# Attention with VectorE, ScalarE and TensorE shifted by one score map

## What is computed

```python
# hybrid mixer: 8 heads, query and key width 96, value width 64, causal
s = jnp.einsum('bqhd,bkhd->bhqk', qi, k[:, :kv_len]) * scale
p = jax.nn.softmax(jnp.where(mask, s, -jnp.inf), axis=-1)
outs.append(jnp.einsum('bhqk,bkhd->bqhd', p, v[:, :kv_len]))

# even layer, differential attention: 4 heads, each with two maps, value width 128
s = jnp.einsum('bqhmd,bkhmd->bhmqk', q_blk, k) + bias[None, :, None]
p = jax.nn.softmax(jnp.where(visible, s, NEG_INF), axis=-1)
w = p[:, :, 0] - lam * p[:, :, 1]
out = jnp.einsum('bhqk,bkhd->bqhd', w, v)
# even layer, band attention: 8 heads of width 64, one map each
p = jax.nn.softmax(s + bias + mask, axis=-1)
out = jnp.einsum('bhnqk,bnkhd->bnqhd', p, vb)
```

## Time and profile before

| | us |
|---|---|
| median of 3 runs | 3531.28 (3527.48 to 3535.3) |
| profiled execution, its own time | 3538.57 |
| its span | 3536.8 |
| TensorE busy | 3287.1 (93%) |
| VectorE busy | 1962.2 (55%) |
| ScalarE busy | 1193.7 (34%) |
| GpSimd busy | 1003.5 (28%) |
| mean granted clock of TensorE over the span | 0.96 |

### The profile page before, as it was taken

One profiled execution on the slowest core, in us unless ns is written; L12 is line 12 of the kernel. 1 busy time (PEld: TensorE's weight loads), 2 busy tenths in 40 slices (PEclk: granted clock), 3 DMA queues, 4 the chain that ended last, 5 costly groups with the idle time before them and its releaser, 6 DMA issues.

```text
span 3536.8 us, 40413 instructions
## 1 busy us (share of the span) xinstructions
PE 3287.1 (93%) x14349; PEld 2589.3 (73%) x14349; DVE 1962.2 (55%) x2865; ACT 1193.7 (34%) x1790; POOL 1003.5 (28%) x713
## 2 busy tenths in 40 slices
PE   6999999999999999998999989988999978599998
PEld 4887875678787888775788767756878857378887
DVE  5565465656545533555655443347676479764443
ACT  3222244432223222425422223354333243143332
POOL 2888000068803700000188400000884021000000
PEclk9999999999999999999999999989999999799999
DMA  6666352166534633330366433202664332023332
GB/s 208 198 195 180 91 133 56 38 178 200 177 96 137 191 95 92 88 85 24 108 199 197 131 89 107 72 1 77 202 194 145 94 103 77 13 82 93 98 95 83
DMA packets 577201, 417.68 MB, mean 118 GB/s; under 512 B 30123, under 2 KB 537370, under 8 KB 575942
## 3 DMA queue, kind: packets, MB, share of 16 engines
q1 hardware_dynamic: 532434, 283.99, 27.4%
q0 software_dynamic: 34304, 121.64, 11.5%
q10 hardware_dynamic: 10356, 10.69, 1.1%
HBM read 408.91 MB, written 6.06 MB: 117 GB/s over the span
## 4 chain that ended last, share of the span: by engine, by line
PE 59%; DVE 16%; POOL 15%; issue 4%; ACT 3%; DMA 2%; ACTq 0%; SPq 0%; DVEq 0%; POOLq 0%
PE bank L324 17%; PE bank L326 17%; PE bank L325 17%; POOL mod_acc L663 8%; POOL mod_w L660 4%; PE bank L1264 2%; PE bank L1295 2%; POOL mod_w L632 2%; DVE tmp L438 2%; DMA mod_w<-in_w_ada 2%; DVE w_lo L305 2%; DVE h_lo L448 1%; POOL mod_acc L666 1%; PE bank L1285 1%; DVE w_lo L296 1%
## 5 line engine op out<-in xcount | busy, mean ns | idle before, releaser
L324 PE MATMUL bank<-h_hi,w_hi 128*128 128x512 f32 x2656 | 1053.5, 397 | 70.3 <-DVE w_lo L305 23.5
L326 PE MATMUL bank<-h_hi,w_lo 128*128 128x512 f32 x2656 | 1043.5, 393 | 0.0
L325 PE MATMUL bank<-h_lo,w_hi 128*128 128x512 f32 x2656 | 1043.3, 393 | 0.0
L305 DVE TENSOR_TENSOR w_lo<-raw,w_hi 128x1024 fp32r<-128x1024 f32 x438 | 660.7, 1509 | 538.1 <-ACT w_hi L288 535.9
L288 ACT ACTIVATE w_hi<-raw 128x1024 fp32r<-128x1024 f32 x438 | 462.1, 1055 | 671.6 <-PE bank L326 668.2
L324 PEld LDWEIGHTS bank<-h_hi,w_hi 128*128 128x128 f32 x2656 | 503.0, 189 | 208.1 <-issue 49.0
L326 PEld LDWEIGHTS bank<-h_hi,w_lo 128*128 128x128 f32 x2656 | 502.8, 189 | 108.4
L325 PEld LDWEIGHTS bank<-h_lo,w_hi 128*128 128x128 f32 x2656 | 503.6, 190 | 103.0 <-issue 0.2
L663 POOL TENSOR_TENSOR mod_acc<-mod_acc,mod_w 128x1024 f32<-128x1024 f32 x168 | 455.7, 2712 | 14.0
L324 PE MATMUL bank<-hid_hi,w_hi 128*128 128x512 f32 x1056 | 416.3, 394 | 15.4 <-DVE w_lo L305 15.3
L326 PE MATMUL bank<-hid_hi,w_lo 128*128 128x512 f32 x1056 | 414.2, 392 | 0.0
(11 more groups left out here) (318 smaller groups left out, 3350.1 us busy)
## 6 DMA issues: line engine op xcount, KB each, us to landing
raw<-in_ffn_w_gu SPq DMA_DIRECT2D x176, 512.0 KB, 4.0
mod_w<-in_w_ada POOLq DMA_DIRECT2D x128, 512.0 KB, 4.0
mod_w<-in_mod_w POOLq DMA_DIRECT2D x96, 512.0 KB, 4.2
raw<-in_ffn_w_in SPq DMA_DIRECT2D x88, 512.0 KB, 3.7
raw<-in_ffn_w_down SPq DMA_DIRECT2D x64, 512.0 KB, 4.0
raw<-in_w_in SPq DMA_DIRECT2D x34, 512.0 KB, 3.7
raw<-in_ffn_w_out SPq DMA_DIRECT2D x32, 512.0 KB, 4.0
raw<-in_ffn_w_down SPq DMA_DIRECT2D x32, 384.0 KB, 3.4
```

The lines of the kernel that those rows point to most:

```text
L305: loop(nc.vector.tensor_tensor(w_lo[:, u % 2, :], raw[:, u % 2, :], w_hi[:, u % 2, :].bitcast(F32), ALU.subtract), "split_lo", times)
L324: nc.tensor.matmul(dst, a_hi, b_hi, start=start, stop=False)
L325: nc.tensor.matmul(dst, a_hi, b_lo, start=False, stop=False)
L326: return nc.tensor.matmul(dst, a_lo, b_hi, start=False, stop=stop)
```

## The change

It shifts VectorE and ScalarE by one map and TensorE's scores by another:

- TensorE issues the scores of maps 0 and 1 at the start. In the turn of map j it transposes map j, issues the scores of map j + 2 and then the outputs of map j. For a map without outputs it only issues the scores of map j + 2.
- VectorE takes map j + 1 and then divides map j.
- ScalarE does the exponentials of map j + 1 and the evacuation of map j - 1 before the copies of map j.
- The latent stages get a third map buffer, `m_probs2`, at `mod_at`, with its slot in `smx`; a buffer is reused after three maps instead of two.

```diff
@@ -1172,6 +1172,7 @@
         m_later = [g[0]]
         m_probs = [place(f"m_probs{i}", [P, 1280], F32, m_later) for i in range(2)]
         m_probs_end = m_later[0]
+        m_probs.append(place("m_probs2", [P, 1280], F32, [mod_at]))
         lat = place("lat", [P, 6, S], F32, g)
         pos = place("pos", [P, S], I32, [g[0]])
         conv_u = place("conv_u", [P, S], F32, g)
@@ -1267,11 +1268,11 @@
 
             outs = [j for j in range(len(jobs)) if "v" in jobs[j]]
             scores(0)
+            scores(1)
             for j in range(len(jobs)):
-                if j + 1 < len(jobs):
-                    scores(j + 1)
                 job = jobs[j]
                 if "v" not in job:
+                    scores(j + 2)
                     continue
                 pb = job["turn"]
                 former = outs.index(j) - 1
@@ -1286,6 +1287,8 @@
                                                   ident[:, :])
                     if kb != 2:
                         done(ins, "probs_turned", (key, j, sig))
+                if j + 2 < len(jobs):
+                    scores(j + 2)
                 if job.get("free") is not None:
                     wait(pe, *job["free"])
                 rows, bank = job["rows"], job["bank"]
@@ -1311,6 +1314,10 @@
             exps(0)
             for j in range(len(jobs)):
                 job = jobs[j]
+                if j + 1 < len(jobs):
+                    exps(j + 1)
+                if j >= 1 and "v" in jobs[j - 1]:
+                    after(act, j - 1)
                 if "v" in job:
                     for g in range(3):
                         wait(act, "probs_turned", (key, j, g))
@@ -1321,12 +1328,9 @@
                         bank, c, _ = TURN_AT[g]
                         done(nc.scalar.activation(pt[:, g, g * P:S], psum[bank][:, c:c + n], ACT.Copy), "turned_read",
                              (key, j, g))
-                if j + 1 < len(jobs):
-                    exps(j + 1)
-                if "v" in job:
-                    after(act, j)
                 if beside is not None:
                     beside(act, j)
+            after(act, len(jobs) - 1)
 
         def attend_dve(dve, key, jobs, minus_lam=None, beside=None):
 
@@ -1366,9 +1370,9 @@
                     dve.wait_ge(sg.sem("probs_ready"), sg.count["probs_ready"])
             scores(0)
             for j in range(len(jobs)):
-                divide(j)
                 if j + 1 < len(jobs):
                     scores(j + 1)
+                divide(j)
                 if beside is not None:
                     beside(dve, j)
 
@@ -1428,8 +1432,8 @@
             for h in range(HEADS):
                 jobs.append(dict(
                     q=lambda i, h=h: q_full[0:HD, h, i * P:(i + 1) * P], k=lambda n, h=h: k_full[0:HD, h, 0:n],
-                    bias=causal, scale=HD ** -0.5, buf=m_probs[h % 2], slot=h % 2, turn=m_probs[h % 2],
-                    after=h - 2 if h >= 2 else None,
+                    bias=causal, scale=HD ** -0.5, buf=m_probs[h % 3], slot=h % 3, turn=m_probs[h % 3],
+                    after=h - 3 if h >= 3 else None,
                     v=lambda kb, h=h: v_tok[:, kb, h * VD:(h + 1) * VD], pt=m_probs_t,
                     rows=slice(VD * (h % 2), VD * (h % 2 + 1)), bank=h // 2 % 2))
             return jobs
```

## The result

| | before | after |
|---|---|---|
| median, us (4 runs each) | 3533.24 | 3565.96 (3554.83 to 3567.55) |
| ratio, 95% interval | | 1.0089 (1.0064 to 1.0113) |
| profiled execution, us | 3538.57 | 3567.20 |
| TensorE busy, us | 3287.1 | 3294.5 |
| mean granted clock | 0.96 | 0.954 |

Slower by 32.7 us: 3566 where 3570 was forecast. The windows view gives the three stages and two periods of four maps in the even stage (start:end, length, busy us of TensorE, its weight loads, VectorE, ScalarE and GpSimd, then clock, DMA share, GB/s). It answers to the earlier trace rows.

What follows compares the result with a forecast made beforehand. TensorE alone was taken to bound the steady latent stage. Two latent stages at +8.6 (+17.2) and the even stage at +21.2 gave +38.4: profiled 3577, median 3570, range 3550 to 3590.

Steps and rivals of the forecast that it cites:

- The ring: Latent stage: transposes, scores, take, divide and hand-offs form a closed cycle, 6.95 us per map against 5.85, +1.10.
- the latent +8.6: Each of two latent stages grows by 8.6 us, bounds +6 and +11; together +17.2.
- The copies' hold: End of a latent stage: outputs of the seventh map wait some 1.3 us for ScalarE's copies, behind exponentials and evacuation.
- The even stage: Even-mixer attention stage of 16 maps: grows by 21.2 us, bounds +12 and +28.
- The first fall: Even stage, after the 3.4 us wait: transposes and scores at half rate, +3.4 per period of four maps.
- The second: Even stage, around one-column sums and 64-row scores: another clock fall, 2.5 us per period, 7.5 in three, between 0 and 4.6.
- The end: End of the even stage: the wait before the last transposes goes, the last outputs are held; +0.5, an estimate.
- A: Rival: small waits pull the clock down through the whole latent stage; +61, or +30 for half the time, 3600; chance 0.08.
- B: Rival: the clock stays up in the even stage, which then costs 3.5; sum +20.7, 3552; chance 0.14.
- C: Rival: faster, VectorE's divide is done in time and TensorE never stops; 3497; chance 0.05.
- D: Rival: no difference, modelled matmul ends hide 1 us of TensorE's work per map; 3538; chance 0.04.
- the earlier exponentials: ScalarE: 2.3 us of exponentials per map, run before the copies, leave every path but the last one.

Runs made afterwards that it cites:

- e6: Changed kernel plus a memset of 1024 unused columns on VectorE behind every take of the latent stages; 3583.86 us, 1.0137 of before.
- e7: Kernel before plus a memset of 1024 unused columns on VectorE behind every take of the latent stages; 3531.69 us, 0.9990 of before.
- e8: Changed kernel plus 12 unused 128-column matmuls in TensorE's 3.3 us wait of the even stage; 3550.72 us, 1.0043 of before.
- e3: Changed kernel with ScalarE's order alone put back; 3567.71 us, 1.0099 of before.
- e5: Kernel before with all three engines advanced by one map only where the next map has no outputs; 3518.92 us, 0.9957 of before.
- e4: Kernel before with only TensorE's new order and the third buffer; 3557.33 us, 1.0068 of before.
- e2: Changed kernel with VectorE's order alone put back, dividing map j before taking j+1; 3543.28 us, 1.0023 of before.

## Why the prediction was right

The direction, the mechanism and the size were right: 3566 against 3570, inside the range. That it came within 4 us is in part luck: the difference was forecast at +38.4 and is +32.7, and 2 of the 5.7 us between were made up by before's median, which a fourth run moved from 3531.3 to 3533.2. The profiled execution was forecast at 3577 and took 3567.2. Point by point:

- **The ring.** Forecast 6.95 us, measured 6.70. Take, divide and the step to TensorE are as summed (616.98 to 618.63, to 620.11, to 620.17: 1.65 + 1.48 + 0.06). The two hand-offs on TensorE's side were each 0.1 too long: the scores start 1.15 after the transposes, where I took the 1.29 after which outputs start, and the take 2.36 after the scores, not 2.46. So each map loses 0.85, not 1.10. e6 and e7 show that VectorE's time is in the cycle now and was not before.
- **Where the latent +8.6 became +7.5.** From the second scores to the second transposes: 11.3 before, 15.6 after, +4.3 (forecast +5.6; the second scores ran at 4.11 rather than 4.64, the third at 2.88 where I charged 3.4, and the rings were shorter). Five rings: 33.5 against 29.4, +4.1 (5.4). From the seventh transposes to the end: 10.2 against 11.2, -0.9, where I had 8.6, -2.6. The copies' hold was 1.33 as forecast (1.3), but the outputs behind it took 3.94: I had not charged the clock for this wait.
- **The even stage.** Forecast +21.2, measured +19.5. To the first transposes +2.8 (3.45). A period at full clock was walked as 7.9 + 6.95 + 12.5 = 27.3. The traces have each step without a fall: 7.82 and 6.89 in e8 (2331.93 to 2339.75 to 2346.64) and 12.42 in e3 (2346.61 to 2359.03), 27.1 together. That is a little less than before's 27.48, not "no less", as I wrote. The first fall was charged 3.4 and cost 3.3 in two periods and 1.7 in one. The second, with the wait for ScalarE's square in front, was charged 2.5 and cost 3.8 in two and 2.1 in one, 9.6 in all against 7.5; this was a guess between bounds. So 17.9 us of the three periods' 99.2 are falls of the clock, nearly as much as the stage's whole +19.5 (before's periods have one fall each too). The end, from the last transposes after a map without outputs, gave +0.4 (0.5).
- **Sum.** +34.4 in the profiled stages, +32.7 in the medians, +38.4 forecast. Most terms were too long (the end of a latent stage and the second fall were too short). The ring's error has one source: hand-offs taken from the neighbouring pair of operations instead of the pair that stands in the new order.

**The rivals.** A (the clock falls all through the latent stage) did not come: granted 0.92 in the stage against 0.91 before, and 1.00 through the five steps with 0.93 us of idle every 6.70. The Trainium skill, "TensorE: Matmul & The Clock Gate", section "A second HAM failure mode: psum-queue depth-cycling", tells of a kernel in which frequent short idles between groups of matmuls make the clock oscillate; here that showed at 1.95 us (e6: one step at 1.00, the next at 0.82) and not at 0.93. B (the clock stays up in the even stage) did not come: 0.76. That e8 with one of the two falls left lands at 3550.7, near B's 3552, is a coincidence, as half of its gain stands in no trace. C (scores in time, so that TensorE never stops) is shut out by the [0.93 <-DVE m_probs] brackets, though e5 shows where there was something to gain. D (no difference) rested on the modelled ends of matmuls hiding the gap. The time itself answers it, 3566 and not 3538, and e8 shows that such idle is real: 2.94 us of additional matmuls fit into a wait of 3.3.

What the forecast did not see is that ScalarE's and VectorE's orders belong together with TensorE's: I treated the earlier exponentials as free. Beside VectorE's new order they are, in sum (e3); but where VectorE divides first and TensorE's scores are ahead, they are worth some 14 us (e4 without them 25 us over before, e2 with them 11).

Three things stay open. Why the clock falls behind the heads' sums in the changed kernel and not in e3 was not settled; by the sum above that is 9.6 us of the loss. One of four runs of the changed kernel took 3554.8 us at a mean clock of 0.961, the others 3564.7 to 3567.6 at 0.953 to 0.954: that fits a run without some of the falls, but only the slower kind has a trace here. And ScalarE's order alone, and with VectorE's, was not run.

## What to carry to other kernels

Before moving a consumer ahead of a producer's last step, write the ring that the new order closes (each operation, each hand-off, taken from the pair that will really stand together) and compare it with the busiest engine's work per turn: here 6.70 against 5.85, which decides the latent stage's steady stretch. Latency that the bounding engine's own work already covers cannot be hidden a second time, so look ahead only where that engine stands in the trace; here that was one map in four. And when a wait on TensorE cannot be removed, price the half rate behind it as well: up to 3.3 us behind a wait of 3.3 here, and in the even stage such falls cost more than the new order itself.

## What the runs showed that I had not expected

- Matmuls that compute nothing of use can pay: 12 of them (24 passes in the trace, 2.94 us) in what was idle took 3.3 us off each of two periods of the changed kernel (e8), whose median fell by 15 us.
- The second scores of a latent stage, behind the same wait of 1.96 us, run mostly at half rate and sometimes at full rate: 4.64 before, 4.11 in the changed kernel, in e2 2.43 in the first stage and 4.63 in the second. Of the twenty such places without filler three ran at full rate. The first latent stage of e7 took 53.1 us and the second 56.2, with the same instructions and waits, by the clock alone: one profile of such a place is one draw, worth up to 3 us.
- The clock falls while TensorE is hardly idle: behind eight passes of one column with 0.18 us of wait in front the scores take 4.62 us, and behind the same eight with no wait (e3) 2.42; both have 0.87 us or so of idle before the transposes ahead. What tells them apart was not tested.
